# The dilated attention loop of a four-block transformer kernel: another order of its steps, strided groups first, and another way to spread a share over a tile

## The reference

```python
B_GROUPS = ((128, 1), (512, 4), (2048, 16))   # S = 512, 8 heads per group, head dim 64
for g, (window, dil) in enumerate(B_GROUPS):
    # scores in blocks of 128 steps of stride dil, with an ALiBi bias; own block and the one before
    o_g, lse_g = dilated_branch(q[:, :, g], k[:, :, g], v[:, :, g], dil, slopes[g])
alpha = softmax(stack(lses), axis=0)           # share of each group, per token and head
o = sum(alpha[..., None] * stack(outs), axis=0)
x = x + o.reshape(B, S, 512) @ b_w_out
```

## Time and profile before

| what | value |
|---|---|
| median of 3 runs | 2745.74 us (2743.84 to 2748.2) |
| the profiled execution, own time | 2742.88 us |
| its span in the trace | 2741.1 us |
| TensorE busy | 2666.0 us, 97% of the span |
| VectorE, ScalarE busy | 1379.5 us, 966.4 us |
| mean granted TensorE clock, share of full | 0.985 |
| the B loop | 858.3 to about 950 us of the span |
| TensorE idle at its start | 864.0 to 867.0 us |
| "bout" behind it | 951.5 to about 978 us |

### The profile page before, as it was taken

One profiled execution on the slowest core, in us unless ns is written; L12 is line 12 of the kernel. 1 busy time (PEld: TensorE's weight loads), 2 busy tenths in 40 slices (PEclk: granted clock), 3 DMA queues, 4 the chain that ended last, 5 costly groups with the idle time before them and its releaser, 6 DMA issues.

```text
span 2741.1 us, 30732 instructions
## 1 busy us (share of the span) xinstructions
PE 2666.0 (97%) x12410; PEld 2148.4 (78%) x12410; DVE 1379.5 (50%) x2089; ACT 966.4 (35%) x1531; POOL 89.4 (3%) x99
## 2 busy tenths in 40 slices
PE   7999999999998799999998999999999999999999
PEld 6867888888888578888874688888888678888887
DVE  5355673664433577466557554334452155544342
ACT  3165442343225444234443443223323142432221
POOL 2000000000000000000010000000020310000000
PEclk9999999999999799999998999999999999999999
DMA  4301233232221022323321023233233022323222
GB/s 144 103 29 39 85 97 111 85 105 97 98 94 63 12 92 93 100 92 100 113 86 39 29 81 106 94 99 100 85 108 118 21 82 95 101 93 100 93 93 92
DMA packets 65518, 237.54 MB, mean 87 GB/s; under 512 B 7408, under 2 KB 7536, under 8 KB 65248
## 3 DMA queue, kind: packets, MB, share of 16 engines
q1 hardware_dynamic: 63648, 229.38, 25.6%
q0 software_dynamic: 1728, 6.19, 0.7%
HBM read 233.45 MB, written 2.10 MB: 86 GB/s over the span
## 4 chain that ended last, share of the span: by engine, by line
PE 93%; DVE 4%; ACT 2%; issue 1%; DMA 0%; SPq 0%; DVEq 0%; ACTq 0%
PE ps L420 28%; PE ps L421 28%; PE ps L422 28%; PE ps L525 2%; PE ps L564 2%; PE ps L545 2%; PE ps L808 1%; PE ps L531 1%; ACT m_B_P L1662 1%; PE ps L795 1%; PE ps L497 0%; PE ps L483 0%; DVE m_wsp L846 0%; DMA m_x<-in_xT 0%; DVE m_B_q L1240 0%
## 5 line engine op out<-in xcount | busy, mean ns | idle before, releaser
L420 PE MATMUL ps<-m_xs,m_wsp 128*128 128x512 f32 x2232 | 880.1, 394 | 22.7 <-DVE m_xs L857 10.7
L421 PE MATMUL ps<-m_xs,m_wsp 128*128 128x512 f32 x2232 | 872.0, 391 | 0.0
L422 PE MATMUL ps<-m_xs,m_wsp 128*128 128x512 f32 x2232 | 871.9, 391 | 0.0
L1560 ACT ACTIVATE m_wsp<-m_raw 128x1024 fp32r<-128x1024 f32 x429 | 446.7, 1053 | 797.3 <-PE ps L422 762.7
L846 DVE TENSOR_TENSOR m_wsp<-m_raw,m_wsp 128x1024 fp32r<-128x1024 f32 x429 | 519.5, 1226 | 208.7 <-ACT m_wsp L1560 208.5
L420 PEld LDWEIGHTS ps<-m_xs,m_wsp 128*128 128x128 f32 x2232 | 421.1, 189 | 117.1 <-issue 21.0
L421 PEld LDWEIGHTS ps<-m_xs,m_wsp 128*128 128x128 f32 x2232 | 421.4, 189 | 89.1 <-issue 2.9
L422 PEld LDWEIGHTS ps<-m_xs,m_wsp 128*128 128x128 f32 x2232 | 421.1, 189 | 88.8
L896 DVE TENSOR_TENSOR m_x<-m_x,ps 128x512 f32<-128x512 f32 x104 | 70.8, 687 | 313.2 <-PE ps L422 313.2
L420 PE MATMUL ps<-m_wsp,m_xs 128*128 128x512 f32 x320 | 125.9, 393 | 0.0
L422 PE MATMUL ps<-m_wsp,m_xs 128*128 128x512 f32 x320 | 125.7, 393 | 0.0
(11 more groups left out here) (308 smaller groups left out, 3225.7 us busy)
## 6 DMA issues: line engine op xcount, KB each, us to landing
m_raw<-in_w SPq DMA_DIRECT2D x429, 512.0 KB, 3.3
m_x<-in_xT SPq DMA_DIRECT2D x4, 512.0 KB, 9.2
m_B_bias<-in_biasB POOLq DMA_DIRECT2D x8, 256.0 KB, 3.1
out<-m_x SPq DMA_DIRECT2D x8, 256.0 KB, 2.3
m_O_D<-in_decay POOLq DMA_DIRECT2D x1, 1024.0 KB, 5.0
m_A_sel<-in_sel POOLq DMA_DIRECT2D x1, 512.0 KB, 3.6
m_E_sel<-in_sel POOLq DMA_DIRECT2D x1, 512.0 KB, 4.0
m_O_cs<-in_ropeo POOLq DMA_DIRECT2D x1, 512.0 KB, 3.7
```

Of the source, the lines that this page charges most:

```text
L420: e.matmul(out, lh, rh, start=first, stop=False)
L421: e.matmul(out, lh, rl, start=False, stop=False)
L422: return e.matmul(out, ll, rh, start=False, stop=final)
L1560: e.activation(wsp[n % NSP][:, 0, :], raw[n % NRAW][:, :], ACT.Copy).then_inc(*s_hi(n))
```

## The change

1. `dilated_units` yields the groups in the order 1, 2, 0, so units 4p and 4p+1 are strided and 4p+2, 4p+3 are group 0.
2. The round of B on TensorE becomes turn(i-2), scores(i), weighted(i-3), among(i). VectorE's becomes turned(i-2), tops(i), among(i), out(i-3), and ScalarE's turned(i-2), exps(i), among(i), out(i-3).
3. The steps of `among` are tied to earlier rounds, `n = i - 4 * p`.
4. The three bfloat16 pieces, their transposes and copy, the table `B_selp` with its two loads and a memset go. `B_spread` takes the share's column itself as the stationary operand, repeated over 64 columns with step zero, and multiplies it by the float32 identity: 8 matmuls of 128x64 by 128x128 for each group, in place of one bfloat16 matmul of 96x128 by 96x512.
5. `B_mix` takes group 1 and 2 first, then group 0. The spreads of p = 3 stand in the last round of the loop; "bout" has no hooks.

```diff
-        for g in range(3):
+        for g in (1, 2, 0):
...
                 for i in range(n + 3):
+                    if 2 <= i <= n + 1 and pre == "B":
+                        turn(units[i - 2])
                     if i < n:
                         spec["before"](units[i])
                         scores(units[i])
-                    spec["among"](i)
                     if i >= 3:
                         weighted(units[i - 3])
-                    if 2 <= i <= n + 1:
+                    spec["among"](i)
+                    if 2 <= i <= n + 1 and pre != "B":
                         turn(units[i - 2])
...
-            def B_alpha(p, kind):
-
-                b = take(kind, "alpha", p)
-                q.wait_ge(*free[b])
-                q.wait_ge(*s_step["pieces", "B", p])
-                for n in range(4):
-                    i = e.transpose(ps[b][:, 0:256].bitcast(BF16)[0:96, 128 * n:128 * n + 128], B_pc[:, n, :], identb[:, :])
...
-                q.wait_ge(*s_soft["alpha", p])
-                q.wait_ge(*d_selp[p // 2]["selp"])
-                e.matmul(ps[b][:, :], B_selp[p // 2][0:96, 3 * (p % 2) + g, :], B_a3[0:96, :], start=True,
-                         stop=True).then_inc(*s_spread((p, g)))
+                q.wait_ge(*s_step["share", p])
+                for n in range(4):
+                    for par in range(2):
+                        share = B_share[:, n, g, 2 * p + par:2 * p + par + 1].broadcast_to([128, 64])
+                        i = e.matmul(ps[b][64 * par:64 * par + 64, 128 * n:128 * n + 128], share, ident[:, :], start=True,
+                                     stop=True)
+                i.then_inc(*s_spread((p, g)))
...
-                    n = i - 4 * p - 3
+                    n = i - 4 * p
                     if n == 2:
                         B_stats(p, "score")
                     if n == 3:
                         B_back(p, "score")
-                    if n == 5:
-                        B_alpha(p, "score")
-                    if n in (6, 7) and p < 3:
-                        B_spread(p, 0 if n == 6 else 2, "score")
-                        if n == 6:
-                            B_spread(p, 1, "score")
+                    if n == 6:
+                        B_spread(p, 1, "score")
+                        B_spread(p, 2, "score")
+                    if n == (7 if p < 3 else 6):
+                        B_spread(p, 0, "score")
...
-                chained(p, 3, e.tensor_tensor(share, share, B_top[:, :, 2:3, h].broadcast_to([128, 4, 3, 2]), ALU.mult))
-                q.wait_ge(*s_zero["B2"])
-                chained(p, 4, e.tensor_copy(piece(0), share))
-                chained(p, 5, e.tensor_tensor(rest, share, piece(0), ALU.subtract))
-                chained(p, 6, e.tensor_copy(piece(1), rest))
-                chained(p, 7, e.tensor_tensor(rest, rest, piece(1), ALU.subtract))
-                e.tensor_copy(piece(2), rest).then_inc(*s_step(("pieces", "B", p)))
+                e.tensor_tensor(share, share, B_top[:, :, 2:3, h].broadcast_to([128, 4, 3, 2]),
+                                ALU.mult).then_inc(*s_step(("share", p)))
...
-                    n = i - 4 * p - 3
-                    if n == 3:
+                    n = i - 4 * p
+                    if n == 4:
                         B_below(p)
-                    if n == 4:
+                    if n == 5:
                         B_shares(p)
                     if n == 6:
+                        B_mix(p, 1)
+                        B_mix(p, 2)
+                    if n == 7:
                         B_mix(p, 0)
-                        B_mix(p, 1)
-                    if n == 7:
-                        B_mix(p, 2)
                     if n == 8:
                         B_split(p)
```

More of the change, by code:

```diff
@@ L388, in build @@
         s_mm, s_stat, s_row, s_score, s_turn, s_pv = (sem(f"s_{n}") for n in ("mm", "stat", "row", "score", "turn", "pv"))
-        s_sums, s_gate, s_tok, s_stats, s_back, s_alpha, s_spread, s_scale = (
-            sem(f"s_{n}") for n in ("sums", "gate", "tok", "stats", "back", "alpha", "spread", "scale"))
+        s_sums, s_gate, s_tok, s_stats, s_back, s_spread, s_scale = (
+            sem(f"s_{n}") for n in ("sums", "gate", "tok", "stats", "back", "spread", "scale"))
         s_hi, s_xhi, s_sq, s_root, s_rowc = (sem(f"s_{n}") for n in ("hi", "xhi", "sq", "root", "rowc"))
@@ L994, in attention @@
                 for i in range(n + 3):
+                    if 2 <= i <= n + 1 and pre == "B":
+                        turned(units[i - 2])
                     if i < n:
@@ L999, in attention @@
                         normalized(units[i - 1])
-                    if 2 <= i <= n + 1 and pre == "B":
-                        turned(units[i - 2])
                     spec["among"](i)
@@ L1240, in B_mix @@
                 e.tensor_tensor(o, o, bank("spread", p, g)[:, :], ALU.mult).then_inc(*s_step(("spread", p, g)))
-                if g:
+                if g != 1:
                     q.wait_ge(*s_step["spread", p, g])
-                    if g == 2:
-                        q.wait_ge(*s_step["mix", p, 1])
-                    e.tensor_tensor(B_q[:, p, :], B_q[:, p, :], o, ALU.add).then_inc(*s_step(("mix", p, g)))
+                    if g == 0:
+                        q.wait_ge(*s_step["mix", p, 2])
+                    a = B_q[:, 4 + p, :] if g else o
+                    e.tensor_tensor(a, B_q[:, 4 + p, :], B_q[:, 8 + p, :] if g else o, ALU.add).then_inc(*s_step(("mix", p, g)))
             def B_split(p):
@@ L1280, in vector_program @@
                                          biased=lambda u: d_bias[min(u.g, 1)]["bias", u.p], out=B_out))
-            B_split(2)
-            B_shares(3)
-            for g in range(3):
-                B_mix(3, g)
+            B_mix(3, 0)
             B_split(3)
@@ L1804, in B_nat_out @@
                 if p:
-                    q.wait_ge(*s_step["pieces", "B", p - 1])
+                    q.wait_ge(*s_step["lse", p - 1, 0])
                 e.activation(B_nat[:, :, 1:3, :, :].rearrange("p n g w h -> p n (g w h)"),
@@ L1813, in B_shares @@
                 e.activation(share, share, ACT.Exp, scale=-1.0).then_inc(*s_soft(("shares", p)))
-            def B_alpha_out(p):
-                q.wait_ge(*s_alpha[p])
-                if p:
-                    q.wait_ge(*s_spread[p - 1, 2])
-                e.activation(B_a3[0:96, :], bank("alpha", p)[:, 0:256].bitcast(BF16)[0:96, :],
-                             ACT.Copy).then_inc(*s_soft(("alpha", p)))
             def B_split(p):
-                q.wait_ge(*s_step["mix", p, 2])
+                q.wait_ge(*s_step["mix", p, 0])
                 e.activation(xs[:, p, 0, :], B_q[:, p, :], ACT.Copy).then_inc(*s_xhi(("bmix", p)))
@@ L2003, in gpsimd_program @@
             for u in B_units:
-                if u.n == 4:
-                    q.wait_ge(*s_mm["bv", 2, 3])
-                    for half in range(2):
-                        load(B_selp[half][:, :, :].bitcast(U16), a["selp"][:, 6 * half:6 * half + 6, :], d_selp[half], "selp")
-                    e.memset(B_pc[:, :, :], 0.0).then_inc(*s_zero("B2"))
-                    q.wait_ge(*s_zero["B2"])
                 if u.first and u.g < 2:
@@ L2110, in host_consts @@
     o["sel"] = bits(sel)
-    selp = np.zeros((128, 12, 128), f)
-    for p in range(4):
-        for g in range(3):
-            for b in (0, 32, 64):
-                selp[b + 8 * g + 2 * p, 3 * p + g, :64] = 1.0
-                selp[b + 8 * g + 2 * p + 1, 3 * p + g, 64:] = 1.0
-    o["selp"] = bits(selp)
     slopes = np.exp2(-8.0 * np.arange(1, 25) / 24).astype(f).reshape(3, 8)
```

22 lines of the change are left out of this document (5 added, 17 removed).

## The result

The changed kernel takes 2716.26 us (median of 4 runs, 2714.57 to 2717.05); the kernel before, run beside it, 2744.79 us (2742.11 to 2748.2). The ratio is 0.9895 with a 95% interval of [0.9877, 0.9912]: 28.5 us faster, about five times the 5.5 us that a measurement can tell from nothing. The forecast was 2732.5, the range 2723 to 2742. The profiled execution took 2716.38 us with a span of 2714.6, 26.5 us less than before.

What follows compares the result with a forecast made beforehand. Loop B was taken as bound by a ring of waits, no engine filling it. Starting k = 3 of "bout" 13.3 us earlier takes the profiled 2742.9 to 2729.6; 2.9 more for the median gives 2732.5 us, range 2723 to 2742.

Steps and rivals of the forecast that it cites:

- The ring: Loop B: engines wait for each other once in two rounds; the new order cuts a pair's period from 22.9 to 19.3 us.
- Its length: Loop B: one pair's period, 18.1 us plus four or five crossings of some 0.25, taken as 19.3 us.
- hand count: Loop B: steps of one pair on TensorE, VectorE and ScalarE summed from profile rows, 18.1 us without crossings between engines.
- Three equal periods: Loop B: scores of unit 2 end at 862.9, those of unit 14 three periods later at 920.8.
- the end: From unit 14's scores at 920.8 to the first "bout" matmul at 939.9 and k = 3 at 948.4, before the start's 2 us.
- The start: Loop B's beginning: no gain there, and some 5 us at half clock cost 2 us, putting k = 3 at 950.4.
- The clock: TensorE in loop B: no pause over 1.5 us, so full clock; granted clock over 0.9 past 872.
- Rival 1: Loop B: one long pause a pair brings half clock back, 21.3 us a pair, 7 us less than now, 2739; chance 0.17.
- the pauses are paid twice: Loop B before: TensorE rests, as from 903.6 to 906.5, then works at 0.50 of the clock for 11.5 us.
- The new spread: TensorE in loop B: 1.02 us a spread, 64 ns a record, 3.06 a pair; the change adds 8 us in all.
- Rival 2: Loop B: step-zero spreads take 1.91 us instead of 1.02, adding 10.7 in all; 3 us gained, 2743; chance 0.06.
- Rivals 3 and 4: Loop B: spreads hold TensorE at half clock, 2753, chance 0.06; VectorE's late mixing returns the period to 23 us, 2744, chance 0.09.

Runs made afterwards that it cites:

- e1: Kernel before with only the new order of steps in a round of loop B, on TensorE, VectorE and ScalarE; 2723.04 us, ratio 0.9925.
- e3: Changed kernel with only the old order of steps in a round put back on the three engines; 2742.89 us, ratio 0.9998.
- e8: Changed kernel with one PSUM bank skipped ahead of "bout" and 10 identity matmuls ahead of the loop's first transposes; 2713.55 us, ratio 0.988.
- e9: Kernel before with 10 identity matmuls ahead of the weighted sums of each pair's first unit, to fill TensorE's long pauses; 2737.94 us, ratio 0.9978.
- e6: Changed kernel with every spread computed twice into the same bank, 192 more records; 2724.45 us, ratio 0.9917.
- e12: Kernel before with the new round order and the new spreading together, groups 0, 1, 2 and mixing steps left where they were; 2724.14 us, ratio 0.9933.
- e13: e12 with the groups in the order 2, 0, 1 and the bias table and statistics held twice; 2724.29 us, ratio 0.9926.
- e5: Changed kernel with groups in the old order 0, 1, 2, mixing steps two rounds later and the last spreads hooked into "bout"; 2713.24 us, ratio 0.9875.
- e2: Kernel before with only the spreading changed: shares spread by the float32 identity, no pieces, alpha or table; 2732.99 us, ratio 0.9965.
- e4: Kernel before with 16 identity matmuls ahead of the first weighted sums of each of the 12 groups; 2764.89 us, ratio 1.0078.

## Why the prediction was right and where it failed

**The ring: right.** The prediction said that loop B is bound by a ring of waits that the order of a round closes, and that the new ring runs over weighted sums, spreads, mixing, copies, exponentials and back to transposes. The chain shows those steps in that order, e1 gets 20.6 of 28.5 us from the order alone, and e3 loses all 28.5 without it.

**Its length: the step that failed.** "With four or five of some 0.25 on the way I take 19.3" is where most of the error sits. The hand count's 18.1 was already too long, and the 1.2 us of crossings came on top of it. Against the chain above: to the end of the third spread 7.2 us, not 8.1 (a spread takes 0.88, where I had counted 1.05 to 1.1, and the eight transposes behind the statistics 0.87, not 1.1); from there to the first exponentials 3.35, not 3.8 (the add 0.61 to the start of the output copy, not 0.75; the copy of the shorter unit 0.47 to the first tops, not 0.7); exponentials, shares and copy 3.9, as counted; transposes and scores 1.9, not 2.3. That makes 16.4. A crossing to another engine costs 0.02 to 0.14 us in the chain, and the 16.4 hold it; between 889.27 and 890.15 stand VectorE's first tops of the next unit, which the listing of the longest pieces leaves out. The allowance of 0.25 each had no row behind it.

**Three equal periods: too many.** From the scores of unit 2 (865.3) to those of unit 14 (912.4) the loop took 47.1 us, I had 57.9. Two periods were 16.4, and the first only 14.3, because no spreads of an earlier pair lie in it, although part of it ran at half clock; I had seen that those are the pair before's, and charged them all the same. The 10.8 us between the two are 3.6 for crossings (three times 1.2), 5.1 for the sizes (three times 18.1 less 16.4) and 2.1 for the first period. They make the bulk of the 12.9 us that k = 3 is earlier than forecast (937.5, not 950.4). Another 2.5 are the end: from the last scores to k = 3 25.1 us, not 27.6, the same short rows again less 0.9 for a longer wait at the bank. The start was 0.4 later than I had it (865.3 for 862.9 + 2.0). 10.8 + 2.5 - 0.4 = 12.9. The median is 16.2 us under the forecast: besides the 12.9, 0.3 lie behind k = 3, and 3.0 come from the step from a profiled execution to the median, which I put at the 2.9 of the kernel before; the changed kernel's profiled execution is 0.1 above its median.

**The clock: right, with its price.** One cold stretch at the start, full clock from 870; I had said over 0.9 past 872. The 2 us for the start was fair (e8: 2.1 earlier at k = 3, 0.5 in the median). Rival 1 did not come: no pause of a pair is over 2.1 us. The prediction's sentence that "the pauses are paid twice" holds for the earlier trace rows, but the second payment is the smaller: e9 puts it at 4.5 us in the median and 6.9 in the loop, and e3 has periods of 22.5 and 21.8 us, the second at full clock throughout.

**The new spread: right in kind, a little dear.** The group of its matmuls in the loop:

```profile
L666 PE MATMUL ps<-m_ident,m_sq 128*64 128x128 f32 x192 | 11.7, 273 | 0.0
```

192 records as counted, 32 of them in 1.75 us in the chain, 55 ns each. The nearest row had given 64. The four passes that the Trainium skill states for true FP32 (FP8 and Floating Point Precision, TensorE Precision Notes) would by the prediction's estimate have been 1.7 us for a spread; the trace shows 0.88, and e6 0.90, so here the measurement decides against it as a price. Rival 2 falls with that. The added work on TensorE is then 12 x 0.88 - 4 x 1.1 = 6.2 us, not 8.

**Rivals 3 and 4: wrong.** The granted clock of the loop is 0.95, not under 0.70. VectorE waits 1.3 us for a spread at most, not 3, and the period is not 23. What e12 and e13 add is that the place of the statistics and the mixing matters by itself: with them a round later three periods take 57.0 us and not the 47.4 of e5. The prediction had no term for that; the change puts the way back a round ahead of `B_below`, and there VectorE's wait for it is gone.

**The range** took the hand period of 18 as its best case and left that count's own error out. Its terms were nearly all rounded up, so their errors add in one direction.

What stays open: how e12's 11.7 us of loop over e5 divide between the wait for the way back, the mixing's round and the lower clock; why the stretches at a lower clock outside the loop come in some kernels' profiled executions and not in others; whether full clock at the loop's start is worth more than 0.5 us of the median.

## What to carry to other kernels

Where several in-order engines pass work round in one loop, write down the ring: who waits for whom in one turn, with the lengths of the steps from the chain. Moving what already can run (here the transposes and their copies) ahead of what must still wait (exponentials, mixing) was worth 20.6 us with not one instruction changed, while filling the pauses to hold the clock was worth 4.5 (6.9 in the loop). When the new ring is summed from rows, take a crossing from a chain too (here 0.02 to 0.14 us), count the first turn by itself, and let the range reach below the hand count as well as above. Gains of two edits on the same ring are not to be added: in the loop 20.8 and 4.2 us alone gave 16.8 together. And before a small gain is put down to an edit, compare the stretches that the edit doesn't touch: of e2's 10.6 us only 4.2 lay in the loop.

## What was not expected of the hardware

A stationary operand with step zero, one column of float32 read 64 times, cost nothing here over the plain one of the weighted sums (64 ns a record): 55 ns a record, two records a matmul of 64 columns by 128, 0.11 us. A float32 matmul of 128x128 by 128x128 with the identity took 0.23 to 0.24 us (16 in 3.6 to 3.8 us in e4, 10 in 2.4 in e9), nearly twice the 0.13 us of a float32 transpose of the same size (8 in 1.06 us in the chain, both at a clock of 1.00); I had taken them as equal when I sized e4.
